# The modulation vectors computed inside the dense layers, and the recurrence's finish rearranged over VectorE, ScalarE and Pool

## The chip, the cores and the metric

One core of one Trainium2 chip runs one program. The time is the device time of one launch in microseconds (us), the median of three runs: 3726.5 before (3725.76 to 3726.89). TensorE (PE) multiplies matrices, VectorE (DVE) and ScalarE (ACT) do elementwise work, Pool (GpSimd) does some elementwise work and can issue DMAs, and SyncE (SP) issues DMAs only.

## The reference, cut to what matters

Two transformer blocks run on 512 tokens of width 1024, all in float32. The first has an RWKV-7 branch and a differential attention branch, a mixture of experts and a gate. The second has two layers (an attention layer and a neighbourhood layer), each with a mixture of experts, over 512 tokens and 256 context tokens. The change touches three pieces of it:

```
# modulation of the second block, for l in 0, 1 (c and c_ctx: 1024 values, ada_w[l]: 1024 x 6144)
mod   = silu(c)     @ ada_w[l] + ada_b[l]      # shift, scale, gate, twice
mod_c = silu(c_ctx) @ ada_w[l] + ada_b[l]
h = rmsnorm(x, g) * (1 + scale) + shift        # where they are used

# finish of the RWKV branch; y: 512 x 8 heads x 64, from the recurrence
y = (y - mean(y)) * rsqrt(var(y) + 64e-5)      # per head
y = y * ln_w + ln_b
out = (y + bonus * v) * g                      # bonus: one value per token and head

# lambda of the differential attention
lam = exp(sum(lq1 * lk1)) - exp(sum(lq2 * lk2)) + lam_init
```

## The kernel before

The program is a list of stages. Each is a function that opens a `Scope` (its own buffers and semaphores) and one `block`, in which every engine has its own written-out list of instructions with semaphore waits. The next stage begins on all engines when every engine has finished its list, DMA waits at its end included. The stages, in order, with the prefix that their buffers bear in the profile: norm `n1` (`n_`); the RWKV projections (`rp_`) and their preparation (`rr_`); `rwkv_chunks` (`rc_`, `ri_`); `rwkv_scan` (`rs_`), the recurrence in 8 chunks of 64 tokens; `rwkv_finish` (`rf_`); dense layer `l1` (`l_`); lambda (`lam_`); heads `h1` (`h_`); attention `a1` (`a_`); sub-norm (`sub_`); two transposes; dense `l3`; a transpose; dense `l5`; experts f1; norm `np`; a transpose (`pq_`); dense `lg`; norm `ne`; dense `le`; heads `he`; attention `ae`; dense `lf`; experts f2; norm `no`; the rest of the odd layer; experts f3; the final norm.

**A dense layer** (`linear_phase`, L353) loops over pieces. A piece is 128 rows by 512 columns of a weight matrix, 256 KB. SP loads it, ACT copies it to a rounded high part (L179), VectorE subtracts to get the low part (L184), and PE makes three matmuls for each 128-token tile (L190 to L192): 12 a piece for 512 tokens, 18 for 768. After the last piece of a column chunk the tiles' sums are read out of PSUM by VectorE or ACT. There are 6 raw buffers, 6 split ones and 8 PSUM banks. Piece n + 6 may be split when PE is done with piece n. In l1 the same SP list also clears 22 MB of `ybuf` in HBM (`Clear.write`), 2 MB behind every third piece.

**The modulation** (`Modulation`, `ModulationSide`, L2433 to L2546) is cut into six parts: layer l, columns g x 2048 to (g + 1) x 2048. A part has eight pieces of 128 x 2048 (1 MB) through a ring of three buffers, four matmuls for each piece (two columns of silu(c) against 512 columns, at partitions 0, 32, 64 and 96 of one bank), a bias group of four, four row copies by ACT, for parts (.,0) and (.,2) on two of the four rows "+ 1" and "times gain" by Pool, and four stores to `modD` in HBM. A part is woven into another stage as `side`: `begin` and `sync` stand at the end of SP's list, `prepare` (silu) ahead of ACT's and `scalar` behind it, `pool` on Pool, and `tensor` puts the matmul groups between the host's own PE work, with a wait for the piece's load in front (L2537). The hosts are h1 (0,0), a1 (0,1), np (1,0), ne (0,2), he (1,1) and no (1,2).

**The norm** (`norm_phase`, L201) works tile by tile: ACT squares and sums, VectorE scales (L311) and shifts (L315), PE transposes (L332), ACT and VectorE split the transposed tile (L179, L184). `n1` is the same function without a part beside it.

**The finish** (`rwkv_finish`, L1635) is one chain on VectorE of ten operations over 128 x 2048 and a few small ones; ACT makes a square root. Pool is idle there and in the scan. **The lambda stage** (`lambda_phase`, L2673) loads four vectors, multiplies and sums them, and takes two exponentials.

Of the kernel before, what the change touches and what calls it, by code (L numbers as in the profile page):

```python
# [200 lines left out]
def norm_phase(nc, name, xs, tab, gain, hT=None, htok=None, mods=None, ahead=None, columns=None, side=None):  # L201

    n = len(xs)
    with Scope(nc, name) as s:
# [18 lines left out]

        extra = side(s) if side else None
# [21 lines left out]
        @block.sync  # L246
        def _(sp):
            for i, (sc, sh) in enumerate(kinds):
                sp.dma_start(SC[i][:, :], bc_row(sc, D)).then_inc(rows_in[i], 16)
                if sh is not None:  # L250
                    sp.dma_start(SH[i][:, :], bc_row(sh, D)).then_inc(rows_in[i], 16)
            if ahead:
                ahead(sp)
            if extra:
                extra.begin(sp)
                extra.sync(sp)

        @block.scalar
        def _(act):
# [21 lines left out]
            if extra:  # L281
                extra.scalar(act)

        if extra:
            @block.gpsimd
            def _(pool):
                extra.pool(pool)
# [34 lines left out]
        if hT is not None:  # L322
            @block.tensor
            def _(pe):
                for t in range(n):
# [10 lines left out]
                    if extra and t < n - 1:  # L336
                        extra.tensor(pe, t, n - 1)
# [15 lines left out]
def linear_phase(nc, name, parts, loads=(), RING=6, RAW=6, ahead=None, clear=None):  # L353


    BANKS = 8
# [21 lines left out]
    with Scope(nc, name) as s:  # L378
# [6 lines left out]
        out_done = {e: s.sem(f"out{e}") for e in "av"}  # L385
        block = s.block()

# [123 lines left out]
def heads_phase(nc, name, tab, items, T, side=None, pool=None):  # L511


    with Scope(nc, name) as s:
# [17 lines left out]
        extra = side(s) if side else None  # L532
# [11 lines left out]
        def _(sp):  # L544
# [4 lines left out]
            if extra:  # L549
                extra.begin(sp)  # L550
                extra.sync(sp)
# [71 lines left out]
        def _(act):  # L623
            if extra:
                extra.prepare(act)
# [12 lines left out]
            if extra:  # L638
                extra.scalar(act)

        if extra:
            @block.gpsimd
            def _(pool):
                extra.pool(pool)

        @block.tensor
        def _(pe):
            for j, (i, t) in enumerate(jobs):
                if mix:
                    mix.tensor(pe, j)  # L650
                if extra:
                    extra.tensor(pe, j, len(jobs))
# [11 lines left out]
def difference_phase(nc, name, tab, qT, kT, value, nlam, o, side=None):  # L664
# [3 lines left out]
    with Scope(nc, name) as s:  # L668
# [12 lines left out]
        extra = side(s) if side else None  # L681
# [4 lines left out]

        if extra:
            @block.sync
            def _(sp):
                extra.begin(sp)  # L690
                extra.sync(sp)

            @block.gpsimd
            def _(pool):
                extra.pool(pool)

        @block.tensor
        def _(pe):
# [29 lines left out]
            for j in range(nj + 3):  # L728
# [6 lines left out]
                if extra and j < nj:  # L735
                    extra.tensor(pe, j, nj)

        @block.scalar
        def _(act):
            if extra:  # L740
                extra.prepare(act)
# [22 lines left out]
            if extra:  # L764
                extra.scalar(act)
# [748 lines left out]
def rwkv_scan(nc, tab, U, KR, Vt, KDt, Bt, PC, y):  # L1514
# [3 lines left out]
    with Scope(nc, "rs") as s:  # L1518
# [7 lines left out]
            s.sem(k) for k in ("st", "rm", "re", "um", "ue", "ysm", "ym", "ye", "sm", "own"))  # L1526
        block = s.block()
        heads = [(h, slice(h * HD, (h + 1) * HD)) for h in range(8)]
# [106 lines left out]
def rwkv_finish(nc, tab, A, y, Vt, bonus, gate):  # L1635

    with Scope(nc, "rf") as s:
        lw = s.sb("lnw", [P, RW])
        lb = s.sb("lnb", [P, RW])
        sq = s.sb("sq", [P, NT, RW])  # L1640
        st = s.sb("st", [P, 3, NT * 8])
        ld, ss, root, own = (s.sem(k) for k in ("ld", "ss", "root", "own"))
# [3 lines left out]
        def _(sp):  # L1646
            sp.dma_start(lw[:, :], bc_row(A["rwkv_ln_w"], RW)).then_inc(ld, 16)
            sp.dma_start(lb[:, :], bc_row(A["rwkv_ln_b"], RW)).then_inc(ld, 16)

        @block.scalar  # L1650
        def _(act):
            act.wait_ge(ss, 1)
            act.activation(st[:, 2, :], st[:, 1, :], ACT.Sqrt).then_inc(root, 1)

        @block.vector
        def _(v):
            link = Chain(v, own)
            y3 = y[:, :, :].rearrange("p t (h d) -> p (t h) d", d=HD)
            q3 = sq[:, :, :].rearrange("p t (h d) -> p (t h) d", d=HD)
            wide = [P, NT * 8, HD]  # L1660
            link(v.tensor_reduce(st[:, 0, :], y3, AX.X, ALU.add))
            link(v.tensor_scalar(st[:, 0, :], st[:, 0, :], 1.0 / HD, None, ALU.mult))
            link(v.tensor_tensor(y3, y3, st[:, 0, :].unsqueeze(2).to_broadcast(wide), ALU.subtract))
            link(v.tensor_tensor(q3, y3, y3, ALU.mult))
            link(v.tensor_reduce(st[:, 1, :], q3, AX.X, ALU.add))
            link(v.tensor_scalar(st[:, 1, :], st[:, 1, :], 1.0 / HD, GN_EPS, ALU.mult, ALU.add))
            v.tensor_copy(st[0:1, 0, 0:1], st[0:1, 1, 0:1]).then_inc(ss, 1)
            v.wait_ge(root, 1)
            link(v.reciprocal(st[:, 1, :], st[:, 2, :]))
            link(v.tensor_tensor(y3, y3, st[:, 1, :].unsqueeze(2).to_broadcast(wide), ALU.mult))  # L1670
            v.wait_ge(ld, 32)
            link(v.tensor_tensor(y[:, :, :], y[:, :, :], lw[:, :].unsqueeze(1).to_broadcast([P, NT, RW]), ALU.mult))
            link(v.tensor_tensor(y[:, :, :], y[:, :, :], lb[:, :].unsqueeze(1).to_broadcast([P, NT, RW]), ALU.add))
            v3 = Vt[:, :, :].rearrange("p t (h d) -> p (t h) d", d=HD)
            link(v.tensor_tensor(q3, v3, bonus[:, :].unsqueeze(2).to_broadcast(wide), ALU.mult))
            link(v.tensor_tensor(y[:, :, :], y[:, :, :], sq[:, :, :], ALU.add))
            link(v.tensor_tensor(gate[:, :, :], y[:, :, :], gate[:, :, :], ALU.mult))

# [767 lines left out]
class ModulationSide:  # L2446
# [32 lines left out]
    def sync(self, sp):  # L2479
        m = self.m  # L2480

        def store(i):
            l, g = self.groups[i]
            sp.wait_ge(self.row_done, 4 * i + 4)
            ready = sum(len(x) for x in self.scaled[:i + 1])
            if ready:
# [21 lines left out]
    def scalar(self, act):  # L2508
        for i in range(len(self.groups)):
            act.wait_ge(self.mm_done, KD * (i + 1))  # L2510
            for q in range(4):
                act.activation(self.row[32 * q:32 * q + 2, i, :], self.ps[i % 2][32 * q:32 * q + 2, :], ACT.Copy
                               ).then_inc(self.row_done, 1)

    def pool(self, pool):
        done = 0
        for i in range(len(self.groups)):
            for q in self.scaled[i]:
                done += 1
                row = self.row[32 * q:32 * q + 2, i, :]  # L2520
                pool.wait_ge(self.row_done, 4 * i + q + 1)
                pool.tensor_scalar(row, row, 1.0, None, ALU.add).then_inc(self.one_done, 1)
                pool.wait_ge(self.one_done, done)
                pool.tensor_tensor(row, row, self.gain[i][32 * q:32 * q + 2, :], ALU.mult).then_inc(self.gain_done, 1)

    def tensor(self, pe, step, steps):
# [5 lines left out]
        for n in range(total * step // steps, total * (step + 1) // steps):  # L2532
            i, k = self.pieces[n]
            ps = self.ps[i % 2]
            if k == 0 and i >= 2:
                pe.wait_ge(self.row_done, 4 * (i - 1))
# [136 lines left out]
def lambda_phase(nc, A, nlam, lam_init):  # L2673

    with Scope(nc, "lam") as s:
        r = s.sb("r", [P, 4, HD])
        d = s.sb("d", [P, 2])
# [466 lines left out]
```

## Time and profile before

| | us |
|---|---|
| median of 3 runs | 3726.5 |
| profiled execution | 3722.31 |
| its span | 3720.4 |
| scan (`rs_`) | 245 to 291 |
| finish (`rf_`) | 291 to 316 |
| dense l1 | 316.5 to 481 |
| lambda | 481 to 488 |
| heads h1 with part (0,0) | 488 to 537 |
| attention a1 with part (0,1) | 537 to 591 |
| dense l3, dense l5 | 611 to 662, 670 to 719 |
| norm np with part (1,0) | 1375 to 1424 |
| dense lg | 1427 to 1488 |
| norm ne with part (0,2) | 1494 to 1540 |
| dense le, heads he with part (1,1) | 1540 to 1626, 1626 to 1687 |
| dense lf | 1786 to 1864 |
| norm no with part (1,2) | 2548 to 2593 |

Over the whole span PE is busy 84%, VectorE 66%, ACT 52%, Pool 16% of the time. The profile gives each instruction's start and duration by engine and by line of the kernel; buffer numbers and digits are left out of names, so that l1, l3 and l5 all appear as `l_`. `PEclk` is the granted TensorE clock as a share of 2.4 GHz.

### The profile page before, as it was taken

The page shows a single profiled execution, that of the slowest core. Times are in us where ns is not written, and L with a number is a line of the kernel's source. Part 1 is how long each engine was busy: PE and PEld are TensorE (multiplying, and loading weights), DVE is VectorE, ACT ScalarE, POOL GpSimd, SP SyncE. Part 2 cuts the span into 40 slices and gives each one's busy share as a digit, 9 for nine tenths or more (in the row PEclk, how much of TensorE's full clock was granted, in tenths as well). Part 3 has the DMA queues.
Part 4 walks back from the last instruction along what each step waited for, and adds up shares of the span by engine and source line. Part 5 has one row for each costly group of instructions (what it writes and reads, how often), then busy time and mean ns, then how long its engine had stood idle before and what let it go on. Part 6 is the DMA issues. An engine that isn't in the chain of part 4 may idle for free. (4 is left out here: it accounts for less than half of the span.)

```text
span 3720.4 us, 49725 instructions
## 1 busy us (share of the span) xinstructions
PE 3118.3 (84%) x18592; PEld 2535.2 (68%) x18592; DVE 2446.7 (66%) x2650; ACT 1930.0 (52%) x2211; POOL 584.4 (16%) x447
## 2 busy tenths in 40 slices
PE   7786957789999947678859999992998859999993
PEld 5685825668888835456648888871776748888873
DVE  3535246479999943455369999975215559999984
ACT  3312334267777732226247777763215537777762
POOL 0220000012222210000002222212004202222211
PEclk9898978889999978789979999995998979999997
DMA  4006642379999952430159999976111249999992
GB/s 125 1 4 227 208 154 77 132 271 366 376 372 370 364 183 103 176 112 11 57 212 373 373 378 383 374 267 225 58 46 27 60 175 383 368 368 363 365 341 103
DMA packets 226547, 830.58 MB, mean 223 GB/s; under 512 B 69686, under 2 KB 94134, under 8 KB 145756
## 3 DMA queue, kind: packets, MB, share of 16 engines
q1 hardware_dynamic: 194572, 784.09, 57.2%
q0 software_dynamic: 31680, 43.92, 3.4%
q8 instruction: 99, 1.62, 0.2%
q10 hardware_dynamic: 144, 0.52, 0.0%
q14 instruction: 52, 0.43, 0.0%
HBM read 814.46 MB, written 85.43 MB: 242 GB/s over the span
## 5 line engine op out<-in xcount | busy, mean ns | idle before, releaser
L184 DVE TENSOR_TENSOR f3e_w_lo<-f_raw,f3e_w_hi 128x2048 fp32r<-128x2048 f32 x198 | 446.3, 2285 | 6.3 <-ACT f3e_w_hi L179 6.3
L184 DVE TENSOR_TENSOR f1e_w_lo<-f_raw,f1e_w_hi 128x2048 fp32r<-128x2048 f32 x192 | 433.0, 2285 | 5.4 <-ACT f1e_w_hi L179 5.4
L184 DVE TENSOR_TENSOR f2e_w_lo<-f_raw,f2e_w_hi 128x2048 fp32r<-128x2048 f32 x192 | 433.4, 2285 | 4.6 <-ACT f2e_w_hi L179 4.6
L179 ACT ACTIVATE f3e_w_hi<-f_raw 128x2048 fp32r<-128x2048 f32 x198 | 371.0, 1910 | 0.3 <-issue 0.3
L179 ACT ACTIVATE f1e_w_hi<-f_raw 128x2048 fp32r<-128x2048 f32 x192 | 360.0, 1910 | 0.0
L179 ACT ACTIVATE f2e_w_hi<-f_raw 128x2048 fp32r<-128x2048 f32 x192 | 359.8, 1909 | 0.0
L190 PE MATMUL l_psum_acc<-l_w_hi,m_hT_hi 128*128 128x512 f32 x288 | 116.1, 403 | 33.3 <-DVE l_w_lo L184 33.3
L184 DVE TENSOR_TENSOR l_w_lo<-l_raw,l_w_hi 128x512 fp32r<-128x512 f32 x70 | 48.2, 692 | 123.3 <-ACT l_w_hi L179 123.2
L2091 POOL DMA_INDIRECT ybuf<-f1e_y,f_dst x32 | 67.9, 2121 | 339.8 <-DVE f1e_y L2297 339.8
L2091 POOL DMA_INDIRECT ybuf<-f3e_y,f_dst x32 | 67.5, 2109 | 341.9 <-DVE f3e_y L2297 331.4
L2091 POOL DMA_INDIRECT ybuf<-f2e_y,f_dst x32 | 67.8, 2118 | 338.4 <-DVE f2e_y L2297 338.4
L179 ACT ACTIVATE l_w_hi<-l_raw 128x512 fp32r<-128x512 f32 x70 | 44.3, 632 | 142.1 <-PE l_psum_acc L192 92.9
L191 PE MATMUL l_psum_acc<-l_w_lo,m_hT_hi 128*128 128x512 f32 x288 | 115.5, 401 | 0.0
L192 PE MATMUL l_psum_acc<-l_w_hi,m_hT_lo 128*128 128x512 f32 x288 | 115.3, 400 | 0.0
L190 PE MATMUL f3e_psum_gate<-f3e_w_hi,f3e_xT_hi 128*128 128x512 f32 x264 | 110.6, 419 | 3.3 <-DVE f3e_xT_lo L184 3.3
L190 PE MATMUL f3e_psum_y<-f3e_w_hi,f3e_hT_hi 128*128 128x512 f32 x264 | 104.7, 396 | 3.7 <-DVE f3e_hT_lo L184 3.7
L190 PE MATMUL f1e_psum_gate<-f1e_w_hi,f1e_xT_hi 128*128 128x512 f32 x256 | 106.3, 415 | 0.0
L190 PE MATMUL f2e_psum_gate<-f2e_w_hi,f2e_xT_hi 128*128 128x512 f32 x256 | 105.5, 412 | 0.0
L192 PE MATMUL f3e_psum_gate<-f3e_w_hi,f3e_xT_lo 128*128 128x512 f32 x264 | 104.8, 397 | 0.0
L190 PE MATMUL f3e_psum_up<-f3e_w_hi,f3e_xT_hi 128*128 128x512 f32 x264 | 102.8, 389 | 2.1 <-DVE f3e_w_lo L184 2.1
L191 PE MATMUL f3e_psum_y<-f3e_w_lo,f3e_hT_hi 128*128 128x512 f32 x264 | 104.4, 396 | 0.0
L191 PE MATMUL f3e_psum_gate<-f3e_w_lo,f3e_xT_hi 128*128 128x512 f32 x264 | 104.4, 395 | 0.0
(819 smaller groups left out, 8836.4 us busy)
## 6 DMA issues: line engine op xcount, KB each, us to landing
f_raw<-in_moe_w_dram SPq DMA_DIRECT2D x390, 1024.0 KB, 7.5
f_raw<-in_w_gate_dram SPq DMA_DIRECT2D x64, 1024.0 KB, 7.9
f_raw<-in_w_up_dram SPq DMA_DIRECT2D x64, 1024.0 KB, 7.3
f_raw<-in_w_down_dram SPq DMA_DIRECT2D x64, 1024.0 KB, 6.6
ybuf<-m_zeros SPq DMA_DIRECT2D x11, 2048.0 KB, 13.7
l_raw<-in_w_in_dram SPq DMA_DIRECT2D x56, 256.0 KB, 9.2
h_adaw<-in_ada_w_dram SPq DMA_DIRECT2D x8, 1024.0 KB, 6.6
a_adaw<-in_ada_w_dram SPq DMA_DIRECT2D x8, 1024.0 KB, 5.0
```

What stands on the lines that cost most here:

```text
L179: return act.activation(dst, src, ACT.Copy)
L184: return v.tensor_tensor(dst, src, hi.bitcast(F32), ALU.subtract)
L190: pe.matmul(out, lh, rh, start=first, stop=False)
L191: pe.matmul(out, lh, rl, start=False, stop=False)
L192: return pe.matmul(out, ll, rh, start=False, stop=last)
L2091: pool.indirect_dma_start(out=ybuf, out_offset=bass.IndirectOffsetOnAxis(ap=R.dst[:, k - 1:k], axis=0), in_=y[:, :], in_offset=None, bound ...
```

## The change

1. A part of the modulation is no longer a `side` of a norm, heads or attention stage. `linear_phase` takes it as `host`: l1 (0,0), l3 (0,1), l5 (0,2), lg (1,0), le (1,1), lf (1,2). Its small loads, its eight 1 MB loads and its stores are issued by Pool. The eight matmul groups stand in front of eight weight pieces, from the fourth on. In l1 the silu stands first in ACT's list. With a host a dense stage has 7 PSUM banks for its sums in place of 8.
2. The "+ 1, times gain" is one VectorE instruction from PSUM; those rows are no longer copied by ACT.
3. During the scan Pool makes AG = (v * bonus + ln_b) * gate and GL = gate * ln_w, four operations for each of four tiles. The finish then has y = (y - mean) * (GL * rstd) + AG, tile by tile, with the squares on ACT.
4. The lambda stage is dissolved into the finish.

```diff
-def linear_phase(nc, name, parts, loads=(), RING=6, RAW=6, ahead=None, clear=None):
-    BANKS = 8
+def linear_phase(nc, name, parts, loads=(), RING=6, RAW=6, ahead=None, clear=None, host=None):
+    BANKS = 7 if host else 8
...
+        extra = host(s) if host else None
+        steps = [3 + m * (min(len(pieces) - 3, 38) - 3) // (KD - 1) for m in range(KD)]
+        rows_at = steps[-1] + 1 + RING
+        if extra:
+            @block.gpsimd
+            def _(pool):
+                extra.begin(pool)
+                extra.sync(pool)
...
+                if extra and n in steps:
+                    extra.tensor(pe, steps.index(n), KD)
                 pe.wait_ge(lo_done, n + 1)
...
+            if extra:
+                extra.prepare(act)
             for n in range(len(pieces) + LAG):
+                if extra and n == rows_at:
+                    extra.scalar(act)
...
+                if extra and n == rows_at:
+                    extra.vector(v)
...
-    def pool(self, pool):
...
+    def vector(self, v):
+        for i in range(len(self.groups)):
+            for q in self.scaled[i]:
+                v.wait_ge(self.mm_done, KD * (i + 1))
+                v.scalar_tensor_tensor(out=self.row[32 * q:32 * q + 2, i, :], in0=self.ps[i % 2][32 * q:32 * q + 2, :],
+                                       scalar=1.0, in1=self.gain[i][32 * q:32 * q + 2, :], op0=ALU.add, op1=ALU.mult
+                                       ).then_inc(self.gain_done, 1)
```

In the scan, on Pool (`link` waits for each instruction before the next):

```diff
+            pool.wait_ge(ld, 32)
+            for t in range(NT):
+                heads = Vt[:, t, :].rearrange("p (h d) -> p h d", d=HD)
+                link(pool.tensor_tensor(AG[:, t, :].rearrange("p (h d) -> p h d", d=HD), heads,
+                                        bonus[:, 8 * t:8 * t + 8].unsqueeze(2).to_broadcast([P, 8, HD]), ALU.mult))
+                link(pool.tensor_tensor(AG[:, t, :], AG[:, t, :], lb[:, :], ALU.add))
+                link(pool.tensor_tensor(AG[:, t, :], AG[:, t, :], gate[:, t, :], ALU.mult))
+                link(pool.tensor_tensor(GL[:, t, :], gate[:, t, :], lw[:, :], ALU.mult))
```

The finish (ACT squares tile t when `cd` counts t + 1, then makes the square root and the exponentials; the lambda's loads are issued at the stage's begin):

```diff
+            for t, e in enumerate(every):
+                v.tensor_reduce(st[:, 0, e], heads(y, t), AX.X, ALU.add).then_inc(own, 1)
...
+            for t, e in enumerate(every):
+                v.tensor_tensor(heads(y, t), heads(y, t), st[:, 0, e].unsqueeze(2).to_broadcast(wide), ALU.subtract).then_inc(cd, 1)
+            for t, e in enumerate(every):
+                v.wait_ge(sd, t + 1)
+                v.tensor_reduce(st[:, 1, e], heads(sq, t), AX.X, ALU.add).then_inc(own, 1)
...
+            v.wait_ge(ld, 64)
+            link(v.tensor_tensor(pr[:, 0, :], r[:, 0, :], r[:, 1, :], ALU.mult))
+            link(v.tensor_tensor(pr[:, 1, :], r[:, 2, :], r[:, 3, :], ALU.mult))
+            v.tensor_reduce(d[:, :], pr[:, :, :], AX.X, ALU.add).then_inc(dd, 1)
             v.wait_ge(root, 1)
             link(v.reciprocal(st[:, 1, :], st[:, 2, :]))
+            for t, e in enumerate(every):
+                link(v.tensor_tensor(heads(GL, t), heads(GL, t), st[:, 1, e].unsqueeze(2).to_broadcast(wide), ALU.mult))
+                link(v.tensor_tensor(y[:, t, :], y[:, t, :], GL[:, t, :], ALU.mult))
+                link(v.tensor_tensor(gate[:, t, :], y[:, t, :], AG[:, t, :], ALU.add))
+            v.wait_ge(ee, 1)
+            link(v.tensor_tensor(nlam[:, :], d[:, 1:2], d[:, 0:1], ALU.subtract))
+            link(v.tensor_scalar(nlam[:, :], nlam[:, :], -lam_init, None, ALU.add))
```

## Rows read from the trace of the kernel before

**Rows 1.** Stretches: bounds in us, busy us (instructions) by engine, clock, DMA share, GB/s.
```profile
330.00:410.00 80.00, 80.00 (x344) 64.26 (x343) 26.92 (x41) 18.35 (x29) 0.00 (x0) 1.00 1.03 381
481.30:488.00 6.70, 0.00 (x0) 0.00 (x0) 1.05 (x5) 1.51 (x3) 0.00 (x0) 0.67 0.08 20
1375.40:1423.90 48.50, 17.69 (x104) 6.07 (x105) 11.29 (x20) 12.95 (x25) 5.50 (x4) 0.64 0.58 212
```

**Rows 2.** Order of instructions, PE and VectorE, norm n1: start, duration, [idle before].
```profile
16.59 3.27 PE L332 MATMUL n_psum_pt<-g_tab,n_h 128*128 128x128 f32 x16 [16.59 <-DVE n_h L311]
...
23.20 1.28 DVE L311 SCALAR_TENSOR_TENSOR n_h<-g_x,n_ss,n_scale 128x1024 f32<-128x1024 f32 x1
...
28.22 0.10 DVE L1153 MEMSET rp_older<- 128x1 f32 x2 [0.35 <-PEq L139]
```

**Rows 3.** Order of instructions, PE, norm np and the stage behind it.
```profile
1381.22 1.97 PE L332 MATMUL np_psum_pt<-g_tab,np_h 128*128 128x128 f32 x8 [37.04 <-DVE np_h L311]
...
1423.90 1.94 PE L492 MATMUL pq_psum_pt<-g_tab,pl_p 128*128 128x128 f32 x8 [10.80 <-PEq L139]
```

**Rows 4.** Order of instructions, norm ne (VectorE) and the next stage (ACT).
```profile
1502.26 1.29 DVE L311 SCALAR_TENSOR_TENSOR ne_h<-g_ctx,ne_ss,ne_scale 128x1024 f32<-128x1024 f32 x1
...
1506.17 1.29 DVE L311 SCALAR_TENSOR_TENSOR ne_h<-g_x,ne_ss,ne_scale 128x1024 f32<-128x1024 f32 x1
...
1539.77 1.67 ACT L179 ACTIVATE le_w_hi<-e_lefirst 128x512 fp32r<-128x512 f32 x3 [6.58 <-PEq L139]
```

**Rows 5.** Order of instructions, norm no (VectorE) and the next stage (SP).
```profile
2556.50 1.28 DVE L311 SCALAR_TENSOR_TENSOR no_h<-g_ctx,no_ss,no_scale 128x1024 f32<-128x1024 f32 x1
...
2593.08 7.12 SPq L1076 DMA_DIRECT2D lo_raw<-in_odd_w_in_dram  x11
```

**Rows 6.** Order of instructions, ACT and VectorE, ends of h1, a1 and he.
```profile
525.36 0.60 ACT L637 ACTIVATE m_kT<-h_psum_pt 128x512 f32<-128x512 f32 x1 [2.13 <-PE h_psum_pt L658]
...
537.41 1.28 ACT L762 ACT_TABLE_LOAD   x1 [9.16 <-PEq L144]
...
586.20 0.37 ACT L747 ACTIVATE m_o<-a_psum_out,a_rsum 128x128 f32<-128x128 f32 x1 [1.25 <-PE a_psum_out L724]
...
591.42 1.28 ACT L2722 ACT_TABLE_LOAD   x1 [2.55 <-PEq L139]
...
1681.26 0.42 DVE L184 TENSOR_TENSOR e_kT_lo<-he_psum_pt,e_kT_hi 128x256 fp32r<-128x256 f32 x1 [1.52 <-ACT e_kT_hi L637]
...
1687.63 1.28 ACT L969 ACT_TABLE_LOAD   x1 [4.10 <-PEq L144]
```

**Rows 7.** Waits in a1, 547 to 587: who for whom, us, times, longest.
```profile
DVE a_psum_score L777 <- PE a_psum_score L705: 5.5, 4, 3.7
```

**Rows 8.** Order of instructions, VectorE: the finish's ends, and four 128x512 operations of l1.
```profile
291.57 2.29 DVE L1661 TENSOR_REDUCE rf_st<-m_BT 128x32 f32<-128x2048 f32 x1 [0.93 <-PEq L139]
...
313.75 2.29 DVE L1677 TENSOR_TENSOR m_gate<-m_BT,m_gate 128x2048 f32<-128x2048 f32 x1
...
366.97 2.48 DVE L2745 COPY m_qkv<-l_psum_acc 128x512 f32<-128x512 f32 x4
```

**Rows 9.** Order of instructions, PE, a1.
```profile
569.45 1.04 PE L2539 MATMUL a_psum_ada<-a_adaw,g_silu_c 128*2 128x512 f32 x8
570.42 0.49 PE L705 MATMUL a_psum_score<-m_kT,m_qT 64*128 64x128 f32 x4
```

**Rows 10.** Pool's scatters (ns min/median/max); silu in h1 and a weight split in lg: ACT.
```profile
L2091 POOL DMA_INDIRECT ybuf<-f1e_y,f_dst x32: 973/2200/2208, 797.7 to 1345.8; - x32
...
493.83 0.22 ACT L2506 ACTIVATE g_silu_c<-h_adac 128x16 f32<-128x16 f32 x1 [4.57 <-DMA h_adac<-in_c_ctx_dram]
...
1438.87 0.63 ACT L179 ACTIVATE lg_w_hi<-pl_lgfirst 128x512 fp32r<-128x512 f32 x1 [2.08 <-PE lg_psum_acc L192]
```

**Rows 11.** One line each, ns min/median/max: VectorE and Pool in the preparation, 140 to 155.
```profile
L1306 DVE TENSOR_TENSOR m_KR<-m_KR,m_pr x4: 1749/1754/1758, 140.8 to 153.1; 128x512 f32<-128x512 f32 x4
L1269 POOL TENSOR_TENSOR rr_a<-rr_a,rr_kk x4: 1644/1650/1655, 140.4 to 152.6; 128x512 f32<-128x512 f32 x4
```

More of the change, by code:

```diff
@@ L197, in bc_row, with norm_phase @@
     return ap.rearrange("(a n) -> a n", a=1).to_broadcast([P, n])
-def norm_phase(nc, name, xs, tab, gain, hT=None, htok=None, mods=None, ahead=None, columns=None, side=None):
+def norm_phase(nc, name, xs, tab, gain, hT=None, htok=None, mods=None, ahead=None, columns=None):
     n = len(xs)
@@ L1665, in _, with heads @@
-            link(v.tensor_reduce(st[:, 1, :], q3, AX.X, ALU.add))
-            link(v.tensor_scalar(st[:, 1, :], st[:, 1, :], 1.0 / HD, GN_EPS, ALU.mult, ALU.add))
-            v.tensor_copy(st[0:1, 0, 0:1], st[0:1, 1, 0:1]).then_inc(ss, 1)
+            def heads(buf, t):
+                return buf[:, t, :].rearrange("p (h d) -> p h d", d=HD)
+            wide = [P, 8, HD]
+            every = [slice(8 * t, 8 * t + 8) for t in range(NT)]
+            for t, e in enumerate(every):
+                v.tensor_reduce(st[:, 0, e], heads(y, t), AX.X, ALU.add).then_inc(own, 1)
@@ L1671, in _ @@
[L1671 to L1676, printed above, removed]
@@ L2847, in early @@
             ahead.fetch(sp)
-        norm_phase(nc, "np", xs, tab, A["norm_ple"], hT=hT, ahead=early, side=lambda s: modulation.side(s, [(1, 0)], 3))
+        norm_phase(nc, "np", xs, tab, A["norm_ple"], hT=hT, ahead=early)
         transpose_phase(nc, "pq", lambda t, k: pt[:, t, k * P:(k + 1) * P], NT, 2, pT, tab)
@@ L2859, in ple @@
         linear_phase(nc, "lg", [linear(operand(hT), KD, allt, A["w_ple_gate"], D, gate_evac, on="a"),
-                                linear(operand(pT), 2, allt, A["w_ple_proj"], D, add, behind=0)], ahead=ahead)
+                                linear(operand(pT), 2, allt, A["w_ple_proj"], D, add, behind=0)], ahead=ahead,
+                     host=lambda s: modulation.side(s, [(1, 0)], 3))
 def gated_add(rows_of, xs, G):
@@ L2902, in even_mixer @@
             norm_phase(nc, "ne", xs, tab, A["norm_mix_g_2"][0], hT=hT, mods=[mods[is_x(t)] for t in range(NTA)],
-                       ahead=ahead.fetch, side=lambda s: modulation.side(s, [(0, 2)], 3))
+                       ahead=ahead.fetch)
             def evac(v, link, ps, t, c):
@@ L2907, in evac @@
                 return v.tensor_copy(pj[:, t, c * 512:c * 512 + n], ps)
-            linear_phase(nc, "le", [linear(operand(hT), KD, lambda c: range(NTA), A["even_w_in_2"], 1280, evac)], ahead=ahead)
+            linear_phase(nc, "le", [linear(operand(hT), KD, lambda c: range(NTA), A["even_w_in_2"], 1280, evac)], ahead=ahead,
+                         host=lambda s: modulation.side(s, [(1, 1)], 3))
         oT = m.pair("oT", [P, 8, NTA * P])
@@ L2929, in even_mixer @@
                          scale=1.0, dst=turned(kT), **common)], NTA * P,
-                    side=lambda s: modulation.side(s, [(1, 1)], 3),
                     pool=lambda s: PoolSide(s, [A["band_x"], A["band_c"]], A["pool_w_2"], A["pool_scale_2"], pooled))
@@ L2936, in even_mixer @@
         linear_phase(nc, "lf", [linear(operand(oT), 8, lambda c: range(NTA), A["even_w_out_2"], D, gated_add(is_x, xs, G))],
-                     loads=[(G[j][:, :], bc_row(mod(j, 2), D)) for j in range(2)])
+                     loads=[(G[j][:, :], bc_row(mod(j, 2), D)) for j in range(2)],
+                     host=lambda s: modulation.side(s, [(1, 2)], 3))
 def odd_pairs(qT, kT, vv):
@@ L2979, in odd_mixer @@
         mods = [(mod(j, 1), mod(j, 0)) for j in range(2)]
-        norm_phase(nc, "no", xs, tab, A["norm_mix_g_2"][1], hT=hT, mods=[mods[is_x(t)] for t in range(NTA)], columns=XT0,
-                   side=lambda s: modulation.side(s, [(1, 2)], 3))
+        norm_phase(nc, "no", xs, tab, A["norm_mix_g_2"][1], hT=hT, mods=[mods[is_x(t)] for t in range(NTA)], columns=XT0)
         qT, kT = q.pair("qT", [P, 8, SEQ]), q.pair("kT", [P, 8, NTA * P])
```

150 lines of the change are left out of this document (45 added, 105 removed).

## The prediction

> **What bounds the kernel now.** I read the share of busy time first, then busy time by stretch, then the order of instructions at the seams between stages. In the expert stages, some 560 us each, nothing is changed. The rest is a string of stages with a barrier behind each, so a stage costs its own longest chain, and work off that chain is free until the stage's last engine is done. The reader should see two kinds of stage. In a dense stage TensorE never stops: 80.00 busy of 80.00 us, at full granted clock [rows 1]. In a norm stage it does little and waits: 17.69 busy of 48.5 us at a granted clock of 0.64 [rows 1]. Six stages carry one sixth of the modulation each (8 loads of 1 MB, 8 groups of 4 matmuls, a bias group, 4 row copies, in four cases Pool's "+1, times gain", a store); the change lifts these sixths from light stages into dense ones.
>
> **What leaves the light stages.** Each term is the next stage's start less the time at which the stage's own work would be done.
> - Norm before the gate (np). The first norm (n1) is the same stage without a load beside it: first transposes at 16.59, next stage at 28.22, so 11.6 us [rows 2]. In np the transposes start at 1381.22 and the next stage at 1423.90, 42.7 us [rows 3]. Between them PE stands for the modulation's weights with the norm's transposes queued behind. Gain 42.7 - 11.6 = 31.
> - Norm with six tiles (ne). The second tile's scaling starts at 1502.26 and the third's at 1506.17, so 3.9 us a tile, VectorE's own work [rows 4]. Four more tiles put the last at 1517.9; 2.6 for its scale and shift, and then 3.7 to the next stage, as in n1 from the end of the last scaling (23.20 + 1.28) to 28.22 [rows 2]: 1524.2. The next stage started at 1539.77 [rows 4]. Gain 15.
> - Norm no, the same from 2556.50 at 4.0 us a tile (its evacuations are in four pieces): last tile 2572.5, next stage from 2579; the next stage's first load was issued at 2593.08 [rows 5]. Gain 14.
> - Heads h1. Its own last copy is 525.36 + 0.60; the next stage's first instruction is at 537.41 [rows 6]. With 0.5 of seam (VectorE idled 0.35 at the seam in rows 2) the gain is 10.9: row copies, four Pool operations, stores.
> - Attention a1. Own end 586.57, next stage 591.42 [rows 6]: 4.3. In its body VectorE waited 5.5 us in four pieces, 3.7 in the longest, for scores that stood behind modulation matmuls [rows 7]; I take 4.4 of it. Together 8.7.
> - Heads he. Own end 1681.68, next 1687.63 [rows 6]: 5.4, with 0.9 for the last transposes that stood behind two modulation groups and 0.7 in the body: 7.
> - The lambda stage goes whole, 6.7 us in which PE did nothing and VectorE 1.05 [rows 1]. Its five small VectorE operations move into the finish (0.8 of them under the wait for the square root, 0.4 behind it, counted below); its loads are long there by then.
> - The finish ran 291.57 to 316.04, 24.5 us, ten large VectorE operations of 2.29 in a chain [rows 8]. After: three rounds of four quarter-size operations unlinked (four take 2.48 [rows 8]), 7.5; twelve linked ones of 0.69 + 0.03, 8.6; small ones 2.1. The squares on ACT (0.6 each) run one tile behind the subtractions, and the square root's table load of 1.3 has VectorE's 2.5 of sums above it. Sum 18.3, gain 6.2. If ACT lagged, at most its last square shows, 0.7.
> Sum of the gains: 31 + 15 + 14 + 10.9 + 8.7 + 7 + 6.7 + 6.2 = 99.5 us.
>
> **What the dense stages pay.** A group of modulation matmuls in a full clock holds PE from 569.45 to 570.42, 0.97 us [rows 9]. Eight and the bias group are 9 x 0.97 = 8.7 us a stage, six stages 52.4. PE is the bound there, so nothing hides it: this is the largest cost. Below, it could be nearly nothing only if PE had gaps, and rows 1 show none; above, the cold group takes about twice, 105 in all. I take the warm price, since the first group comes at the fourth weight piece, some ten us into the stage.
>
> The loads go from SP's queue to Pool's, with 4 to 8 small loads ahead of the first large one. The trace has no plain load issued by Pool. Its scatters took 0.97 at least and 2.20 in the median [rows 10]. I take 1.0 for a small load of one to two rows (nearest to the least, which has the fewest rows) and 1.6 for a 1 MB one. From Pool's start to the first weights there are then 4 x 1.0 + 1.6 + 5.5 of landing = 11 us, or 13 with the two gains, 17 in l1. PE comes to the fourth piece 12 to 18 us into the stage: in lg at 1438.87, when ACT was let go by the third piece's end, 12 us in, the tightest [rows 10]. Waits: 1.1 in lg, 1 in l1, little elsewhere; 2.5 in all. At 2.2 an issue they would be 35 (a rival). The ring of three is ample after that: a load has three steps, 10 us or more.
>
> In l1 the silu of c now stands first in ACT's queue, ahead of the first weight split. In h1 ACT stood 4.57 us for them [rows 10], behind other loads; in l1 they are Pool's first, and ACT would wait some 3 for weights anyway. Cost 1.6, bounds 0 and 4.6, once. l1 also has a full DMA: share 1.03, 381 GB/s while it clears ybuf [rows 1]. The 8 MB are 21 us of DMA more; the clearing ends near 410 and PE at 480, so all of it fits, but the first 3 MB come when the weights' lead is least (7 weight pieces split against 3 used, 8 or 9 us). Half the rate for 3 MB delays SP's queue by 8 us, and with 7 PSUM banks in place of 8 the first evacuations have no whole chunk to spare. I take 2.5, bounds 0 and 10.
> The Trainium skill, DMA: Bandwidth & Descriptors, section Queues, rings and completion order, says each DMA engine takes turns among the queues that have work, packet by packet. No row here shows two heavy queues at once. By that rule the delay in l1 is the 8 us of halved rate; by strict order of arrival it would be nearer 3, and the sum 5 us apart at most.
>
> The stores: rows are complete three pieces before a stage's end (8.2 us in a stage of 512 tokens) and PSUM evacuation follows; copies 2.4, four issues, landing 2.5: 8.9. Only le, whose last pieces are half as wide, shows some: 1.
>
> **The scan.** Pool does 16 operations of 128x512 while it runs, 21 us or more of its 45. The state product on VectorE has both inputs in SBUF. Where such an operation met a Pool operation before, it took 1.75 us, where 0.69 is usual for the shape [rows 8, 11]; so it can lose up to 1.08. It sits on the scan's edge, where PE waited for the state already. Four or five of eight chunks meet Pool; at half the loss, 2.2 us. Bounds: 0, and 16 (every VectorE operation of five chunks at 1.08).
> The Trainium skill, SBUF — State Buffer, section Who interferes with whom, has a narrower rule: a VectorE instruction with two SBUF inputs contends with a Pool instruction that reads SBUF, one with a PSUM input does not. That speaks against this change and names just one of the chunk's three operations. By it the upper bound would be 5, by rows 11 alone it stays 16.
>
> **Sum.** Costs 52.4 + 2.5 + 1.6 + 2.5 + 1 + 2.2 = 62.2. Net 99.5 - 62.2 = 37 us less. The profiled execution took 3722.31 (span 3720.4 and 1.9 around it), so 3685 on its scale; the median of the runs is 4.2 above it, so 3689.
>
> **The rivals.**
> - *Pool's issue is dear, and the change is slower.* Every DMA that Pool issues costs the 2.2 us of the median scatter [rows 10]. Then the first weights come 16.5, 21 or 27 us into the stages: waits of 10 (l1), 5 (l3), 8 (l5), 9 (lg), 0.5 and 2.4, 35 in all. A PE that stood still that long ran at half clock in np [rows 1], and a piece at half clock costs 2.4 more in five stages: 12. Stores: 5. Costs 62 - 2.5 + 52 = 112 against 99.5: 12 slower, 3738. For it: the median row. Against: those rows carry 128 rows and an index list each. It decides from about 1.9 us an issue. 7%.
> - *The clock stays low where the matmuls left.* The modulation kept PE busy in a1 and he. If PE stayed at the low level (1.2 GHz) through a1, its remaining 7.6 of each 9.95 us would double to 15, 5 a cycle, four cycles, 20; he some 3. Net 14 less, 3712. For it: PE's clock is low in every light stage [rows 1]. Against: at the low level PE has no gaps in a1, and such stretches rose. 13%.
> - *The matmuls cost less than their turn, or the norms gain more*: groups between dense matmuls overlapping with their ends. At 0.75 a group costs fall by 12: 3677. 10%.
> - That the work doesn't do what it says (moves but leaves the seams) has no case: no light stage keeps any of it.
>
> **How the numbers follow.** The sum as worked out 70%, 3689, own range 3677 to 3703. With the clock rival in, and small errors in eight gains, 3669 to 3713 leaves out the slow rival, half of the clock one's far side and a tail below. A change of 0.2% is 7.5 us, about what can be told here. Faster 0.89 (70 + 13 + 10, less 4 for their tails), same 0.05 and slower 0.06 (the slow rival and those tails).
>
> **What would show it.** np from first transposes to the next stage's start at 11 to 12 us; ne and no 30 long; h1 to a1 with no gap beyond a microsecond. Dense stages longer by 8.7 to 11, with 72 modulation matmuls in each and PE without gaps save before the first group. Pool's issues near 1 us. The state product at 0.43 in late chunks and up to 1.5 in early ones. The prediction fails if modulation groups take 1.5 us or more among dense matmuls, if PE idles over 5 us before a first group, or if a1 takes longer than its 50 us.

## The result: 24.7 us less, where 37 were forecast

The changed kernel took 3702.0 us in the median of 4 runs (3701.0 to 3703.4) against 3726.7 before: ratio 0.993, 95% interval 0.9915 to 0.9945. The forecast was 3689 with a range of 3669 to 3713, so sign and range hold. The size fell short by a third, and that is what the experiments were for.

The profiled execution took 3700.99 (span 3698.7), 21.3 less than that of before. By stage, from one stage's start to the next one's, in us (lambda stands with the finish, its 6.7 taken out of l1's row):

| stage | change | forecast |
|---|---|---|
| np, ne, no | -30.9, -13.6, -14.9 | -31, -15, -14 |
| h1, a1, he | -11.2, -8.3, -7.2 | -10.9, -8.7, -7 |
| finish and lambda | -6.6 - 6.7 | -6.2 - 6.7 |
| l1 | +17.7 | +13.8 |
| l3, l5, lg, le, lf | +11.8, +9.3, +11.7, +11.6, +10.6 | 8.7 each, 2.5 more among them |
| scan | -1.9 | +2.2 |
| stages not touched | +6.9 in sum | 0 |

The gains came to 99.3 against 99.5. The dense stages cost 72.7 against 60.0. That l3 pays 11.8 and l5 9.3 for the same work is the clock at their starts: ahead of the first group l3 lost 1.2 us more to half-clock matmuls than in the kernel before, and l5 1.2 less.

Stretches of the changed kernel (bounds, busy us and instructions by engine, clock, DMA share, GB/s): l1, l3, and np whole.

```profile
320.00:410.00 90.00, 85.38 (x372) 64.74 (x370) 26.12 (x41) 17.06 (x27) 2.64 (x5) 0.95 1.04 403
605.00:655.00 50.00, 50.00 (x248) 33.03 (x247) 18.62 (x28) 8.03 (x13) 4.65 (x9) 1.00 0.51 196
1381.10:1398.70 17.60, 7.61 (x32) 6.41 (x32) 11.10 (x20) 10.69 (x21) 0.00 (x0) 0.50 0.35 104
```

np is 17.6 us long in place of 48.5 [rows 1]. l3 still has a PE without gaps. l1 has not: 85.38 busy of 90, where it was 80.00 of 80.00 [rows 1].

The changed kernel's order of instructions: np's first transposes and the next stage (answering rows 2 and 3), the ends of h1 and a1 (rows 6), and the finish from its first to its last large operation (rows 8).

```profile
1387.18 3.67 PE L320 MATMUL np_psum_pt<-g_tab,np_h 128*128 128x128 f32 x16 [35.79 <-DVE np_h L299]
...
1398.77 0.44 PE L495 MATMUL pq_psum_pt<-g_tab,pl_p 128*128 128x128 f32 x1 [1.68 <-PEq L139]
...
530.49 0.60 ACT L634 ACTIVATE m_kT<-h_psum_pt 128x512 f32<-128x512 f32 x1 [2.12 <-PE h_psum_pt L646]
531.35 1.28 ACT L735 ACT_TABLE_LOAD   x1 [0.27 <-PEq L139]
...
576.47 0.37 ACT L720 ACTIVATE m_o<-a_psum_out,a_rsum 128x128 f32<-128x128 f32 x1 [2.16 <-PE a_psum_out L701]
577.10 1.28 ACT L2693 ACT_TABLE_LOAD   x1 [0.27 <-PEq L139]
...
292.31 1.28 DVE L1660 TENSOR_REDUCE rf_st<-m_BT 128x8 f32<-128x512 f32 x2 [0.94 <-PEq L139]
...
309.10 0.69 DVE L1681 TENSOR_TENSOR m_gate<-m_BT,m_AG 128x512 f32<-128x512 f32 x1
```

From np's first transposes to the next stage are 11.6 us, as in n1 [rows 2]. Behind the last copies of h1 and a1 the next stage starts within 0.3 us, where rows 6 have 11.5 and 4.9. The finish ends at 309.8, 17.5 us after its start, and two small operations follow.

**Where the cost is: one group among dense matmuls.** PE in l3 of the changed kernel:

```profile
623.64 0.39 PE L191 MATMUL l_psum_acc<-l_w_lo,m_orT_hi 128*128 128x512 f32 x1
623.87 0.39 PE L192 MATMUL l_psum_acc<-l_w_hi,m_orT_lo 128*128 128x512 f32 x1
624.19 1.04 PE L2541 MATMUL l_psum_ada<-l_adaw,g_silu_c 128*2 128x512 f32 x8
625.16 0.50 PE L190 MATMUL l_psum_acc<-l_w_hi,m_orT_hi 128*128 128x512 f32 x1
625.50 0.40 PE L191 MATMUL l_psum_acc<-l_w_lo,m_orT_hi 128*128 128x512 f32 x1
625.73 0.39 PE L192 MATMUL l_psum_acc<-l_w_hi,m_orT_lo 128*128 128x512 f32 x1
```

Dense matmuls follow each other at 0.227. The group starts 0.32 after its forerunner, and the second dense matmul behind it comes 0.34 after the first. From 623.87 to 625.73 are 1.86 us where three steps take 0.68, so the group adds 1.18. Between group starts at 609.72 and 613.63 there is one piece of 2.72 us, which leaves 1.19; over two pieces (617.55 to 624.19) 1.20. The prediction had taken the 0.97 that lie between 624.19 and 625.16. Summed over a stage (every step above 0.227 around a group) eight groups and the bias cost 10.5 to 10.6, not 8.7.

**l1's second cost.** PE's waits in l1, and the order around the longer one:

```profile
PE l_psum_acc L190 <- DVE m_qkv L2716: 4.6, 2, 2.7
```

```profile
345.17 1.97 ACT L179 ACTIVATE l_w_hi<-l_raw 128x512 fp32r<-128x512 f32 x3 [7.62 <-DMA l_raw<-in_w_in_dram]
345.83 2.03 DVE L184 TENSOR_TENSOR l_w_lo<-l_raw,l_w_hi 128x512 fp32r<-128x512 f32 x3 [7.56 <-ACT l_w_hi L179]
...
347.78 2.48 DVE L2716 COPY m_qkv<-l_psum_acc 128x512 f32<-128x512 f32 x4
348.52 0.76 PE L190 MATMUL l_psum_acc<-l_w_hi,m_hT_hi 128*128 128x512 f32 x1 [2.65 <-DVE m_qkv L2716]
349.93 0.63 PE L190 MATMUL l_psum_acc<-l_w_hi,m_hT_hi 128*128 128x512 f32 x1
```

It is read backwards. PE waits for a bank; VectorE copies it out late because three splits stand ahead of the copy in its queue; these waited for ACT, and ACT 7.62 us for a weight piece. Behind the wait PE's matmuls are 0.63 long instead of 0.39, 8 of them: the granted clock is 0.50 from 348.6 to 352.0. Both waits take 5.0 us in sum and the slow matmuls behind them 3.5. The stage also ends 1.3 us later behind its last matmul than in the kernel before (2.2 against 0.9), with a clearing of semaphores (L143) and a second barrier there that l1 of before doesn't have.

**Pool's issues and its work in the scan.** Pool in l3, and the first chunk of the scan:

```profile
597.54 1.95 POOL L2478 DMA_DIRECT2D l_adab<-in_ada_b_dram  x4 [146.10 <-POOLq L139]
599.47 1.62 POOL L2503 DMA_DIRECT2D l_adaw<-in_ada_w_dram  x3
...
254.05 0.42 DVE L1620 TENSOR_TENSOR rs_tmp<-rs_psum_S,rs_state 128x256 f32<-128x256 f32 x1 [0.78 <-PE rs_psum_S L1547]
254.51 0.75 DVE L1621 TENSOR_TENSOR rs_state<-rs_tmp,m_PC 128x256 f32<-128x256 f32 x1
255.06 1.33 POOL L1516 TENSOR_TENSOR m_AG<-m_AG,m_gate 128x512 f32<-128x512 f32 x1
255.41 0.68 PE L1541 MATMUL rs_psum_R<-rs_state,m_KR 64*64 64x64 f32 x16 [0.48 <-DVE rs_state L1621]
```

Pool issues a small load in 0.49 us in these rows (0.75 for the first in l1) and one of 1 MB in 0.54. No PE wait for a modulation weight is recorded in any dense stage of the changed kernel; the longest delay of a first group is 0.1 us, in lg. In three kernels below (mod_only, l1_late, light_back) l5's first group comes 0.5 to 0.8 late. The state product takes 0.75 once and 0.53 three times beside Pool, 0.42 without; the operation with a PSUM input keeps its 0.42.

### The profile page after: what moved, and what is told of

It is laid out like the page before. It is cut to its first block and busy times, and to the rows that moved or that the text cites. A ratio compares the mean times of both kernels' runs of the same rounds, so it can differ in the third digit from the quotient of the medians.

```text
span 3698.7 us, 49747 instructions
## 1 busy us (share of the span) xinstructions
PE 3136.5 (85%) x18592; PEld 2550.2 (69%) x18592; DVE 2444.4 (66%) x2671; ACT 1928.4 (52%) x2207; POOL 634.2 (17%) x553
## 5 line engine op out<-in xcount | busy, mean ns | idle before, releaser
L192 PE MATMUL f3e_psum_up<-f3e_w_hi,f3e_xT_lo 128*128 128x512 f32 x264 | 103.7, 393 | 0.0
```

Of the source, the lines that this page charges most:

```text
L192: return pe.matmul(out, ll, rh, start=False, stop=last)
```

## The experiments

Each is timed against the kernel before on the same chip, medians in us.

**1. The two halves apart.** mod_only takes `rwkv_scan`, `rwkv_finish` and `lambda_phase` from before; fin_only takes them from the changed kernel and all else from before.

> The kernel before with parts 1 and 2 of the change alone (modulation in the dense stages); scan, finish and lambda stage as before. Theory: the parts add up. In the changed kernel the finish took 17.9 us where 24.5 was, and the lambda stage's 6.7 us went, so without them this kernel is 13 us above it: 3702 + 13 = 3715. Rival (the finish's gain hides in something later, or l1's long waits come from what the finish leaves running): 3708 or less. l1 should show its two waits for PSUM banks (3.04 and 2.36 us between two matmuls) again; if they are gone, they came from the new finish.

> The kernel before with parts 3 and 4 alone (Pool's products in the scan, the finish by tiles, no lambda stage); modulation as before. Theory: 6.6 + 6.7 us less, 3713.5. The scan's length tells two readings apart: in the changed kernel it took 44.0 us against 45.95, at a granted clock of 1.00 against 0.93 in these 46 us. If Pool's work beside it costs time and the clock was chance, the scan takes 46.5 here (VectorE's state product 0.1 to 0.3 longer in the first five chunks) or 44, whichever clock it meets; if Pool's work itself shortens it, it is 44 in this run too and in every other with Pool's products.

mod_only 3714.8 (ratio 0.9966, 0.9954 to 0.9977), fin_only 3710.8 (0.9959, 0.9945 to 0.9973). The halves save 11 and 15 us, together 26 against 24.7. Both halves hold the moved column of experiment 6, some 4.4 us, so halves that add up exactly would give 29; the 3 us between are within what mod_only's runs spread over (3706 to 3716). l1 in mod_only has its waits for banks again (4.03 and 1.34 between two matmuls). fin_only saves 2 more than its two terms: its l1 is 5.0 shorter, which experiment 6 takes up. The scan's length goes with the granted clock, not with Pool: at a mean of 1.00 it takes 43.8 to 44.1 in the five kernels with Pool's products and 43.3 in banks7 and nlam_outer below, which have none; at 0.93 it takes 46.2 to 46.9 in four kernels with them and 45.9 in before and mod_only. So Pool's products cost 0.3 to 1.0. Over these nine kernels the first state product that meets Pool took 0.53 to 1.38, the next ones 0.52 to 0.55.

**2. Groups cut to one small matmul.**

```diff
-            for q in range(4):
-                mm = pe.matmul(ps[32*q:32*q+2, :], sT[:, :, k], W[n % ring][:, 512*q:512*q+512], start=(k == 0), stop=False)
+            if k == 0: ...   # as before
+            else: mm = pe.matmul(ps[0:2, 0:8], sT[:, :, k], W[n % ring][:, 0:8], start=False, stop=False)
```

> The changed kernel, where seven of the eight modulation groups of each dense stage are one matmul over 8 columns in place of four over 512 (what is left out: 7/8 of the modulation's products). All loads, waits and places stay. In the changed kernel a group lengthened the row of dense matmuls by 1.20 us, while it lies 0.97 in the trace of PE. Theory A (0.97 its own streaming, 0.23 for going from the one kind of matmul to the other and back): a place still costs 0.3, so 7 x 0.9 = 6.3 us a stage and 38 in all go: 3664. Theory B (all of the 1.20 is streaming, also the late start of the next matmul): a place costs under 0.1: 46 less, 3656. In l1, theory A and B alike: the two waits of 3.04 and 2.36 us come from late weight loads and stay. Rival for l1: they come from PE's order with the groups in it and go, some 8 us less in l1 with its cold matmuls.

```profile
611.42 0.39 PE L192 MATMUL l_psum_acc<-l_w_hi,m_orT_lo 128*128 128x512 f32 x1
611.74 0.20 PE L2545 MATMUL l_psum_ada<-l_adaw,g_silu_c 128*2 128x8 f32 x2
611.86 0.50 PE L190 MATMUL l_psum_acc<-l_w_hi,m_orT_hi 128*128 128x512 f32 x1
612.20 0.40 PE L191 MATMUL l_psum_acc<-l_w_lo,m_orT_hi 128*128 128x512 f32 x1
612.43 0.40 PE L192 MATMUL l_psum_acc<-l_w_hi,m_orT_lo 128*128 128x512 f32 x1
```

From 611.42 to 612.43 are 1.01 against 0.68: a place costs 0.33 with almost nothing in it (l3 of tiny, rows above). Theory A, with a larger share for the place than it said. The six stages were 4.6 to 5.8 shorter (7 x 0.86 = 6.0, less some cold matmuls), 30.5 in sum. The total, 3621, is no measure of it: with the altered modulation the third router chose other experts, and f3 split 192 weight blocks instead of 198 and was 42 us shorter. Without that it would be 3663, close to theory A's 3664, but some 8 of these 39 us lie in stages that the edit leaves alone; theory A rests on the rows. l1 kept its two waits (6.1 in sum), so PE's order with full groups in it is not their cause.

**3. Eight groups at four places.**

```diff
-        steps = [3 + m * (min(len(pieces) - 3, 38) - 3) // (KD - 1) for m in range(KD)]
+        steps = [4 + m * (min(len(pieces) - 3, 38) - 4) // 3 for m in range(4)]
-                    extra.tensor(pe, steps.index(n), KD)
+                    extra.tensor(pe, steps.index(n), 4)
```

> The changed kernel with its eight groups at four places, two behind each other, in all six dense stages. Theory A (0.97 us of streaming a group, and 0.23 a place for entering and leaving): four places less, 0.9 us a stage, 5.5 in all, 3696.5; the step from one group to the next inside a pair is 0.97. Theory B (a group costs 1.20 wherever it stands): 3702, and a pair lengthens the row by 2.4. In the reduced groups of 'tiny' a place with one matmul over 8 columns still cost 0.35 to 0.4, which speaks for A.

```profile
621.13 0.39 PE L192 MATMUL l_psum_acc<-l_w_hi,m_orT_lo 128*128 128x512 f32 x1
621.45 1.90 PE L2541 MATMUL l_psum_ada<-l_adaw,g_silu_c 128*2 128x512 f32 x16
623.28 0.50 PE L190 MATMUL l_psum_acc<-l_w_hi,m_orT_hi 128*128 128x512 f32 x1
623.62 0.40 PE L191 MATMUL l_psum_acc<-l_w_lo,m_orT_hi 128*128 128x512 f32 x1
623.86 0.39 PE L192 MATMUL l_psum_acc<-l_w_hi,m_orT_lo 128*128 128x512 f32 x1
```

3690.9 (0.9905, 0.9888 to 0.9921), 11 less than the changed kernel: better than A. The pair takes 2.73 - 0.68 = 2.05; one group takes 1.18 to 1.20; so a second one adds 0.85 to 0.87, and a place costs 0.34 beside it. Summed over a stage, the groups cost 9.2 here and 10.5 in the changed kernel, so 4 places less give 1.4 a stage, 8 in all; the other 3 us of the 11 are not explained. 9 x 0.86 + 8 x 0.34 = 10.5 is the changed stage again. The 0.97 of the trace was 0.86 of work and a third of the price of changing over. What in the change costs it isn't shown: dense and modulation matmuls differ in precision (fp32r against fp32) and in the width of the loaded operand (128 columns against 2), and no run varies the one without the other. The trace of a1 before speaks for the precision: there the neighbours load 128 columns too but are fp32, and the step into the group (569.25 to 569.45, 0.20) and the one behind the first matmul after it (0.21) are no longer than the row's others (0.17 to 0.21).

**4. Part (0,0) late in l1.**

```diff
+                if at: pool.wait_ge(mm_done, last[at[0] - 8])      # at = (34, 50)
                 extra.begin(pool)
...
-            if extra: extra.prepare(act)
             for n in range(len(pieces) + LAG):
+                if extra and at and n == at[0]: extra.prepare(act)
```

> The changed kernel, where part (0,0) comes later in l1: its loads start when PE is done with piece 26, its groups stand before pieces 34 to 50 (after most of the clearing), and the silu stands behind 34 weight splits on ACT instead of ahead of all. l1 in the changed kernel: first matmul 7.1 us after the stage's start (4.2 in the kernels without a part there), two waits of 3.04 and 2.36, 3.4 us of half-clock matmuls behind them. Theory: the two waits come from the 8 MB meeting the clearing, so they go, and so does the late start: l1 10 to 11 us shorter, 169 to 170 in place of 180.3, and 3691 in all. Rival (the groups' order or the 7 banks stall PE wherever they stand): only the 2.9 of the start go, 3699.

3689.8 (0.9901, 0.9884 to 0.9918). l1 took 168.8 from first issue to last instruction against 180.3; its first matmul came 4.1 after the start (7.1 before); no wait for a bank is left. Of the 11.5, 3.0 were the late first matmul (the silu ahead of the weight splits on ACT), 5.0 the waits, 3.5 matmuls at the low clock. The edit moves loads, groups and silu together; experiments 2 and 5 take the groups and the loads apart.

**5. Which of two makes l1 wait: late weights or the missing bank?** banks7 is the kernel before with `BANKS = 7` in l1. loads8 is fin_only with eight idle 1 MB loads on Pool:

```diff
+            def _(pool):
+                for n in range(KD):
+                    if n >= 3:
+                        pool.wait_ge(aw_in[n % 3], 16 * (n // 3))
+                        pool.wait_ge(mm_done, last[steps[n - 3] - 1])
+                    pool.dma_start(aw[n % 3][:, :], extra_w...[n, :, 0:2048]).then_inc(aw_in[n % 3], 16)
```

> The kernel before with 7 PSUM banks in l1 in place of 8, nothing else. One corner of four (loads beside the clearing or not, 7 or 8 banks). Theory (the waits in l1 need both, late weights and a bank short): no change, 3726, no wait over 1 us between l1's matmuls. Rival (the missing bank alone): l1 has waits at its column ends, up to 7 us more. A side question: in the kernel before, l1's matmuls followed each other at 0.2333 us, in every other kernel so far at 0.2267 (4.4 us in l1); if it is this program's buffer layout, it shows again here, if chance of an execution, it may not.

> The kernel with the new scan and finish only (fin_only, 3710.8), where Pool also issues eight 1 MB loads of the modulation in l1, in the rhythm of the changed kernel, which nothing uses (part (0,0) is computed in h1 as before), with 8 PSUM banks. Theory 'a bank short decides': weights come late as in the changed kernel, but with a whole chunk of banks free PE does not wait: l1 stays at 159 to 160, 3711. Rival 'late weights decide': PE waits about 5 us and runs 3 more at half clock, l1 at 166 to 167 and 3718.

banks7 3726.8 (0.9997, 0.9987 to 1.0008): nothing. loads8 3713.5 (0.9961, 0.9948 to 0.9973) against fin_only's 3710.8 (0.9959): the totals don't tell the two apart, and the reading rests on the rows of one execution each, with l1 at 164.8 against 158.9 to the last matmul. Who waited in its l1:

```profile
ACT l_w_hi L179 <- DMA l_raw<-in_w_in_dram: 98.7, 20, 11.5
...
PE l_psum_acc L190 <- DVE l_w_lo L184: 27.2, 4, 23.4
```

With 8 banks and no group at all PE waits (3.8 us in three waits past the first), now for the split weights themselves. So late weights make PE wait without a bank short. With the bank short, in the changed kernel, the waits are named after it and take 5.0. The corner with 7 banks, the loads and no group was not run; tiny, with an eighth of the groups' work, is nearest to it (6.1). The expectation had favoured the bank and was wrong, and its rival's 3718 was too high. Weights are late because the eight loads meet the clearing: past its first wait ACT waits 87.2 us for weights here and 39.0 in fin_only's l1, and the clearing's 2 MB writes land after 16.3 us in the median in place of 13.7. The sum of ACT's waits is not a price by itself: nlam_outer, without loads in l1, has 43, and its PE never waits. It takes the clearing too: l3 of the changed kernel has the same eight loads beside its weights at a DMA share of 0.51, and PE has no gap there. The Trainium skill (DMA: Bandwidth & Descriptors, Queues, rings and completion order) says that each DMA engine goes round the queues that have work for it, a packet at a time. The trace agrees in so far as the weights' queue loses when Pool's queue has work; who had how many turns is not shown.

**6. A pace of l1's matmuls that nobody had changed on purpose.**

```diff
-            nlam = q.sb("nlam", [P, 1])
+        nlam = m.sb("nlam", [P, 1])       # ahead of clear and hT
```

> The kernel before, where the 4-byte column nlam is allocated in the mixer's outer scope, ahead of hT, as in the changed kernel, and nothing else. l1's matmuls followed each other at 0.2333 us in the kernel before and in banks7, at 0.2267 in the seven kernels that have nlam in the outer scope. Theory (the place of l1's buffers sets the pace): 0.2267 here, l1 4.4 us shorter, about 3722. Rival (something else in those kernels, the new finish or the moved parts): 0.2333 and no change, 3726.

3721.4 (0.9983, 0.9972 to 0.9994). The same stretch of l1 in three kernels, before, banks7 and nlam_outer:

```profile
410.00:470.00 60.00, 60.00 (x259) 48.20 (x258) 13.86 (x20) 20.44 (x33) 0.00 (x0) 1.00 0.33 90
```

```profile
410.00:470.00 60.00, 60.00 (x259) 48.20 (x258) 13.86 (x20) 19.87 (x33) 0.00 (x0) 1.00 0.31 84
```

```profile
410.00:470.00 60.00, 60.00 (x266) 49.70 (x265) 13.16 (x19) 18.24 (x31) 0.00 (x0) 1.00 0.32 91
```

259 matmuls against 266 in 60 us at full granted clock. The changed kernel moved this 4-byte column too, and so gained some 4.4 us in l1 that hide part of the new costs. What moves is hT and not l1's weight buffers: as built, the column takes 32 bytes of a partition, so hT starts 32 bytes higher, at 48096 in place of 48064, while l1's weight buffers, which had the column ahead of them before too, stay where they were (the first high part at 158688). So in the kernel before the two operands of l1's matmuls start at different remainders of 64 bytes, and here at the same. The other stages fit that: in l3 and l5 (which reads hT again) both operands move by 32 bytes together and the pace is 0.227 in both kernels, and in the RWKV projections the remainders differ before and after the move and the pace is 0.233 both times. That the remainders set the pace is an inference from these stages; no run was made for it.

**7. Moving three parts back.** The parts (0,0), (0,1) and (1,1) stand in h1, a1 and he again, in the form of before; l1, l3 and le have no part and 8 banks.

```diff
-                         host=lambda s: modulation.side(s, [(0, 1)], 3))      # l3
+                             side=lambda s: modulation.light(s, [(0, 1)], 3)) # a1; h1 and he likewise
```

> The changed kernel with parts (0,0), (0,1) and (1,1) back in h1, a1 and he (in the form of before), while (1,0), (0,2) and (1,2) stay in the dense stages lg, l5 and lf. Theory (each stage's cost adds up, as measured in the changed kernel): h1 +11.2, a1 +8.3, he +7.2 = 26.7 back; l1 -16, l3 -11.8, le -11.6 = -39. Net 12 to 13 less: 3689. Rival (PE's time is spent either way, so moving these three is neutral): 3702. A third way (the light hosts' gains were from the clock, and come back as more): above 3705.

3680.7 (0.9879, 0.9862 to 0.9895), 21 less than the changed kernel. h1 +11.0, a1 +8.7, he +5.6; l1 -22.1 to its last matmul, l3 -10.5, le -12.1. l1 gives back more than the 16 expected, since the 16 had been read against a kernel whose l1 ran slower for another reason (6). So by their stages three of the six moves lost time. np, ne and no had paid 59 us for their parts, and the dense stages take these for 32; h1, a1 and he had paid 27, and the dense stages took 41.

**8. What the runs point to.** best_dense: part (0,0) late in l1, three places a stage, the bias added by VectorE instead of by a ninth group. best: the same, with (1,1) back in he.

```diff
+        lo, hi = at or (6, min(len(pieces) - 3, 38))
+        steps = [lo, (lo + hi) // 2, hi]
...
+                    v.scalar_tensor_tensor(out=row, in0=ps, scalar=1.0, in1=row, op0=ALU.add, op1=ALU.add).then_inc(self.one_done, 1)
+                    v.wait_ge(self.one_done, done)
+                    v.tensor_tensor(row, row, self.gain[i][32 * q:32 * q + 2, :], ALU.mult).then_inc(self.gain_done, 1)
+                else:
+                    v.tensor_tensor(row, ps, row, ALU.add).then_inc(self.row_done, 1)
```

> The changed kernel with part (0,0) late in l1 (as in l1_late), the groups at three places instead of eight in every dense stage, and the bias added by VectorE instead of by a ninth group. By the runs so far a group streams 0.86 and a place costs 0.34 more, so a stage pays 8 x 0.86 + 3 x 0.34 = 7.9 in place of 10.57: 2.7 less in six stages, 16, and l1's 11: 3675. If the price of a place grows with the number of groups behind it, or three 1 MB loads for the first place come late, it stays above 3682.

> The same with part (1,1) back in he. In light_back he paid 5.6 us for it, and le pays 7.9 here with what goes with it: 2 less than best_dense, 3673. If he's price is the same as le's: equal.

best_dense 3677.3 (0.9863, 0.9847 to 0.9879); best 3666.9 (0.9832, 0.9818 to 0.9846), 60 us below the kernel before and 35 below the changed one. A stage now pays 7.9 for its groups, as worked out (8.8 in lf). In le the part costs 9.5 with its tail (VectorE's four row operations and Pool's stores behind the last piece), in he 5.3; that makes 4 of the 10 us between the two kernels, and the other 6 are not from one place.

## Why the prediction was right, and where it was short

- *What leaves the light stages*: right term by term, 99.3 against 99.5, the worst ne with 13.6 for 15. Measuring each from the next stage's start to the end of the stage's own work held for all six, with n1 as the pattern for the three norms.
- *What the dense stages pay*: the step that failed. "0.97 a group, 9 x 0.97 = 8.7" should have been 10.6, 63.4 in six stages for 52.4. The 0.97 came from a1, where both neighbours were other small fp32 matmuls [rows 9]; among the dense ones a place costs 0.34 on top of 0.86 a group (experiments 2 and 3). Its rival, 0.75 a group, is refuted.
- *l1's contention and silu*: 4.1 forecast, 10.1 to 11.5 measured (2.9 or 3.0 for the start, 5.0 of waits, 2.2 or 3.5 at the low clock, against before or against l1_late). It was inside the bounds given, 0 to 14.6. The term for the low clock behind each wait was missing, and so was the 1.3 at the stage's end.
- *Waits for the first modulation weights*: 2.5 forecast, none measured. Pool issues in 0.5, not 1.0 and 1.6, and the rival of the dear issue falls with it. The prediction's 17 us for l1 didn't follow from its own terms either: eight small loads at 1.0, 1.6 and 5.5 are 15.
- *Scan*: 0.3 to 1.0 in place of 2.2. The 2 us that it gained were its clock, which is luck. The Trainium skill (SBUF — State Buffer, Who interferes with whom) says that a VectorE operation with two SBUF inputs contends with a Pool operation that reads SBUF, and one with at most one SBUF input doesn't, outside the 2-port perf modes. The rows agree: 0.53 and 0.75 against 0.42 for the state product, nothing for its neighbour with a PSUM input.
- *The low clock in a1 and he*: refuted, a1 took 45.8 and was right to 0.4.
- *Not seen*: the pace of l1's matmuls, 4.4 us in favour. That is luck: without it the change would have saved 20, still inside the range.
- The rest, 6.9 us more in stages that the change leaves alone, is mostly the preparation (+2.8) and f2 (+4.2); the odd layer's +3.9 and f3's -3.9 cancel. Other kernels have these or not; it is left open. In the profiled executions the forecast was 15.6 too high: 12.7 in the dense stages, 6.9 here and 0.2 in the gains, less 4.1 in the scan.

## What to carry to other kernels

A light stage that waits for its side work and a dense stage that never waits are not two ends of one good move: price both for each piece. Here work that cost a light stage 14 to 31 us was worth moving to PE for 9 to 12, work that cost 7 to 11 was not, as the change had it. The price is not fixed: in best_dense and best, l1 takes its part for 9 to 10 (against light_back's l1), less than the 11 that h1 pays for it. Put foreign matmuls into a dense row in few, long blocks, and keep large loads away from a stretch in which the DMA engines are full.

## What was not expected of the hardware

- Breaking a row of fp32r matmuls (128x128 operand loaded, 512 columns) with a block of fp32 ones (128x2 loaded) costs 0.33 to 0.34 us, whether the block is one matmul of 8 columns or two groups of four with 512.
- The same dense row ran at 0.2333 or 0.2267 us a matmul at a granted clock of 1.00, by the place of its buffers: another buffer of 4 bytes, allocated ahead of one operand, decided it (l1 in two kernels against eleven).
- A plain 1 MB load is issued by Pool in 0.54 us, its indirect scatters in 2.12 on average in f1.
